# The third channel group of a depthwise convolution moved from TensorE to GpSimd

## The reference

```
val, gate = split(conv_in)                    # 512 channels each
c = val * sigmoid(gate)                       # the gated product
c = depthwise_conv(c, dw_w, width 31, causal) + dw_b
c = silu(layernorm(c, ln_g, ln_b))
yb = c @ w_conv_out
merged = sigmoid(gate_a) * ya + sigmoid(gate_b) * yb      # ya: state-space branch
h = h + merged @ w_out
```

## Time and profile before

| | |
|---|---|
| median of 3 runs | 1172.03 us (1171.83 to 1173.54) |
| profiled execution, its own time | 1168.89 us |
| its span, first to last instruction | 1167.1 us |
| TensorE busy | 990.0 us, 85% |
| VectorE busy | 320.3 us, 27% |
| ScalarE busy | 131.2 us, 11% |
| GpSimd busy | 14.9 us, 1%, 26 instructions |
| memory traffic | 434.87 MB, mean 373 GB/s |
| mean granted TensorE clock | 0.932 |

### The profile page before, as it was taken

How to read it: one execution, slowest core, us unless ns; L and a number is a source line. 1 busy time by engine, 2 the same in 40 slices (tenths; PEclk the granted TensorE clock), 3 DMA queues, 4 the chain that set the end, 5 groups by cost and what they waited for, 6 DMA issues and landing times.

```text
span 1167.1 us, 23860 instructions
## 1 busy us (share of the span) xinstructions
PE 990.0 (85%) x10044; PEld 462.9 (40%) x10045; DVE 320.3 (27%) x949; ACT 131.2 (11%) x292; POOL 14.9 (1%) x26
## 2 busy tenths in 40 slices
PE   8999999999966667689999997699776997977695
PEld 6887886433422222224444332243222342422242
DVE  5999943421211111112212211122111211111112
ACT  2211230500000000000000000000000000000002
POOL 1111000000000000000000000000000000000000
PEclk9999999999998887879999998799878999997898
DMA  9763687695999999997999999999999999999994
GB/s 260 233 169 110 224 331 287 251 424 233 427 427 424 429 424 427 426 427 301 422 411 399 426 426 427 426 425 427 426 425 426 426 426 426 426 426 428 425 426 195
DMA packets 69355, 434.87 MB, mean 373 GB/s; under 512 B 15232, under 2 KB 31552, under 8 KB 36560
## 3 DMA queue, kind: packets, MB, share of 16 engines
q1 hardware_dynamic: 69184, 434.41, 90.9%
q10 hardware_dynamic: 144, 0.09, 0.1%
HBM read 431.69 MB, written 1.05 MB: 371 GB/s over the span
## 4 chain that ended last, share of the span: by engine, by line
PE 45%; DMA 41%; DVE 9%; SPq 3%; issue 2%; ACT 0%; ACTq 0%; DVEq 0%
DMA ring<-in_w_gate_up 24%; PE ps L1478 17%; DMA ring<-in_w_down 13%; PE ps L1491 8%; DMA early<-in_w_gate_up 3%; PE ps L1444 3%; PE ps L1362 2%; PE ps L1413 2%; PE ps L1224 2%; PE ps L1435 2%; PE ps L1467 2%; SPq L369 2%; SPq L366 1%; PE ps L1460 1%; PE ps L1378 1%
## 5 line engine op out<-in xcount | busy, mean ns | idle before, releaser
L1478 PE MATMUL ps<-ring,base 128*32 128x512 f32 x2208 | 294.3, 674 | 115.8 <-DMA ring<-in_w_gate_up 99.4
L1478 PEld LDWEIGHTS ps<-ring,base 128*32 128x32 f32 x2208 | 74.1, 117 | 307.2 <-issue 156.3
L1491 PE MATMUL ps<-ring,base 128*32 128x256 f32 x2944 | 177.5, 381 | 11.5 <-DMA ring<-in_w_down 11.1
L1491 PEld LDWEIGHTS ps<-ring,base 128*32 128x32 f32 x2944 | 89.7, 110 | 101.6 <-issue 33.4
L1131 DVE TENSOR_SCALAR base<-ps 128x256 f32<-128x256 f32 x46 | 19.5, 425 | 379.6 <-PE ps L1478 379.6
L1224 PE MATMUL ps<-ring 128*128 128x256 f32 (+1 forms) x448 | 103.4, 390 | 0.0
L1224 PEld LDWEIGHTS ps<-ring 128*128 128x128 f32 x448 | 84.9, 192 | 15.8 <-issue 1.4
L697 ACT ACTIVATE base<-base 128x256 f32<-128x256 f32 x46 | 19.1, 416 | 628.5 <-DVE base L1131 628.5
L1087 DVE TENSOR_TENSOR base<-ps,base 128x256 f32<-128x256 f32 x47 | 20.0, 425 | 203.3 <-PE ps L1453 203.3
L1478 PE MATMUL ps<-early,base 128*32 128x512 f32 x368 | 52.4, 694 | 16.3 <-DMA early<-in_w_gate_up 16.3
L1478 PE MATMUL ps<-late,base 128*32 128x512 f32 x368 | 50.1, 666 | 13.6 <-DMA late<-in_w_gate_up 13.6
(11 more groups left out here) (323 smaller groups left out, 687.4 us busy)
## 6 DMA issues: line engine op xcount, KB each, us to landing
ring<-in_w_gate_up SPq DMA_DIRECT2D x96, 2048.0 KB, 38.8
ring<-in_w_down SPq DMA_DIRECT2D x63, 2048.0 KB, 40.6
late<-in_w_gate_up SPq DMA_DIRECT2D x16, 2048.0 KB, 40.5
early<-in_w_gate_up SPq DMA_DIRECT2D x16, 2048.0 KB, 39.8
ring<-in_w_in SPq DMA_DIRECT2D x14, 1024.0 KB, 7.8
ring<-in_w_out SPq DMA_DIRECT2D x4, 1024.0 KB, 13.0
ring<-in_w_s_lin SPq DMA_DIRECT2D x2, 1024.0 KB, 6.1
ring<-in_w_s_gate SPq DMA_DIRECT2D x2, 1024.0 KB, 5.4
```

What stands on the lines that cost most here:

```text
L1478: ins = nc.tensor.matmul(ps[BS * q:BS * q + BS, 0, :].rearrange("p (a c) -> p a c", a=2), xT[:, k % 2, k // 2, :], row[:, :, QW * q:QW * q ...
L1491: ins = nc.tensor.matmul(ps[BS * q:BS * q + BS, 1, 0:QW], actT[:, n % 2, n // 2, :], row[:, out_cols(q)], start=(n == 0), stop=(n == KT - ...
```

## The change

`PM` goes from 3 to 2, so groups 0 and 1 stay on TensorE, and `conv(2)` and `tap_matrices(2)` are gone. Group 3 stays on VectorE. Group 2 is computed by GpSimd right behind the gated product: one `tensor_scalar` for tap 0 with the bias, and for each of the other 30 taps a `tensor_scalar` into one of two scratch tiles and a `tensor_tensor` that adds it to the sum, each waiting for the one before. `tap_matrices(1)` comes after all of it in GpSimd's list. The table of taps now has two groups in a buffer of its own, and its two transfers are issued before SyncE waits for `glu`, ahead of the 16 copies. `mean()` also waits for the new semaphore `conv_pool`.

```diff
-PM = MT - 1
+PM = MT - 2
...
+        taps_sb = sb("taps_sb", [P, 2 * TAPS + 2 * S])
...
-        taps = view(rX2, 128, TAPS)
+        taps = view(taps_sb, 0, 2, TAPS)
+        tapped = [view(taps_sb, 2 * TAPS + S * n, S) for n in range(2)]
...
-                   20: [("conv", 1)], 21: [("out", 1), ("in", 3), ("conv", 2)], 23: [("out", 2)],
+                   20: [("conv", 1)], 21: [("out", 1), ("in", 3)], 23: [("out", 2)],
...
+            for n in range(2):
+                sp.dma_start(taps[:, n, :], T["conv_dw_w"][0].rearrange("j o c -> (j o) c")[
+                    :, (PM + n) * P:(PM + n + 1) * P].rearrange("j p -> p j"), allow_slow_non_contiguous=True
+                             ).then_inc(taps_in, 16)
             sp.wait_ge(glu, 1)
...
             load(N_IN - 1)
-            sp.dma_start(taps, T["conv_dw_w"][0].rearrange("j o c -> (j o) c")[:, PM * P:].rearrange("j p -> p j"),
-                         allow_slow_non_contiguous=True).then_inc(taps_in, 16)
...
             nc.gpsimd.tensor_tensor(cin[:, :, HALO:HALO + L], cin[:, :, HALO:HALO + L], cgate, ALU.mult
                                     ).then_inc(glu, 1)
+            pool.wait_ge(taps_in, 32)
+            pool.wait_ge(glu, 1)
+            acc = cacc[:, PM, :]
+            link(nc.gpsimd.tensor_scalar(acc, cin[:, PM, 0:S], taps[:, 0, 0:1], colp[:, 12 + PM:13 + PM], ALU.mult, ALU.add))
+            for j in range(1, TAPS):
+                link(nc.gpsimd.tensor_scalar(tapped[j % 2], cin[:, PM, j:j + S], taps[:, 0, j:j + 1], None, ALU.mult))
+                nc.gpsimd.tensor_tensor(acc, acc, tapped[j % 2], ALU.add).then_inc(conv_pool, 1)
+                pool.wait_ge(conv_pool, j)
             for m in range(1, PM):
                 pool.wait_ge(conv_mm, m)
                 tap_matrices(m)
...
-            dve.wait_ge(taps_in, 16)
+            dve.wait_ge(taps_in, 32)
...
             def mean():
                 pe.wait_ge(conv_sb, PM)
                 pe.wait_ge(conv_dve, 1)
+                pe.wait_ge(conv_pool, TAPS - 1)
```

More of the change, by code:

```diff
@@ L275, in build @@
                                                                   sem("tap_in"), sem("shifts"), sem("cw_ready"))
-        taps_in, conv_dve = sem("taps_in"), sem("conv_dve")
+        taps_in, conv_dve, conv_pool = sem("taps_in"), sem("conv_dve"), sem("conv_pool")
         scales, dn_tail = sem("scales"), sem("dn_tail")
@@ L962, in _ @@
             recurrence(3)
-            dve.wait_ge(taps_in, 16)
+            dve.wait_ge(taps_in, 32)
             dve.wait_ge(glu, 1)
-            last = cacc[:, PM, :]
-            link(nc.vector.tensor_scalar(last, cin[:, PM, 0:S], taps[:, 0:1], colp[:, 12 + PM:13 + PM], ALU.mult, ALU.add))
+            last = cacc[:, MT - 1, :]
+            link(nc.vector.tensor_scalar(last, cin[:, MT - 1, 0:S], taps[:, 1, 0:1], colp[:, 11 + MT:12 + MT], ALU.mult,
+                                         ALU.add))
             for j in range(1, TAPS):
-                ins = nc.vector.scalar_tensor_tensor(last, cin[:, PM, j:j + S], taps[:, j:j + 1], last, ALU.mult, ALU.add)
+                ins = nc.vector.scalar_tensor_tensor(last, cin[:, MT - 1, j:j + S], taps[:, 1, j:j + 1], last, ALU.mult,
+                                                     ALU.add)
                 if j < TAPS - 1:
```

## The result

The change makes the kernel slower: 1215.49 us in the median of 4 runs (1213.87 to 1219.73) against 1172.2 (now four runs too), a ratio of 1.0374 with a 95% interval of 1.0348 to 1.0399. That is 43.3 us more; 40 were forecast, and the time lies inside the range.

A forecast was written before the change was run, and what follows sets the result against it. Two nearly equal chains, on VectorE and TensorE, were taken to bound the mixer. A delay of 38.7 us through `conv(1)` plus 1.6 for the clock restart made 40.3 on 1172.0: 1212 us, range 1196 to 1232.

The forecast's parts named there:

- The step that decides: On TensorE, `conv(1)` waits for `tap_matrices(1)` behind GpSimd's taps: start at 142.7 instead of 100.26, everything later 38.7 us late.
- What the change removes: `conv(2)` leaves TensorE, 3.6 us worth nothing by itself; `tap_matrices(2)` goes, with one hold of 1.70 us on VectorE.
- The start of the taps: GpSimd's taps need both tables of taps, forecast to be there at 73.5 us, bounds 66 and 76.
- The price of a GpSimd `tensor_scalar`: Each 128x256 tap instruction of this form: 0.40 us, bounds 0.21 and 0.63, from a select at 8 and 128 elements.
- What VectorE loses: GpSimd and VectorE exclude each other in turns, 61 against 61: VectorE loses 25.5 us, bounds 14.6 and 38.
- The sum of the two: Taps on GpSimd end after VectorE's own 41.8 us plus 25.5 us of holds from 73.5, at 140.8 us.
- The second rival, dear GpSimd instructions: GpSimd's form with a factor per partition costs 1.0 us more in each of 31: 1243 us; chance 0.12.
- The restart: TensorE, idle for over 30 us before `conv(1)`, resumes at a slower clock: 1.6 us added, bounds 0 and 3.2.
- 1 to 1 to the end: The experts on TensorE follow without slack, nothing can be fetched ahead, so all of the delay reaches the end.
- The literal lock: Shared ports held for whole GpSimd instructions: VectorE would lose full durations, 29.2 us, and the end would be 1216, not 1212.

The follow-up runs named there:

- the run with tap 0 alone: The changed kernel with taps 1 to 30 of the GpSimd group left out, so part of the computation is missing; 1170.38 us, with 3 blocks of experts more.
- the run with `tensor_tensor`: The changed kernel with each tap's product as a tensor_tensor with the tap broadcast along the row, in place of tensor_scalar; 1209.55 us, ratio 1.0324.
- the matrices first: The changed kernel with a matrix buffer per TensorE group and group 1's tap matrices written ahead of GpSimd's 61 tap instructions; 1182.09 us, ratio 1.0098.
- the convolution last: The changed kernel with the second convolution before the last projection tile in TensorE's and ScalarE's order, not before the ninth from the end; 1187.05 us, ratio 1.0133.
- both edits: The changed kernel with group 1's tap matrices ahead of the taps and the product of each tap as a tensor_tensor; 1188.96 us, ratio 1.0148.
- 98 products: The changed kernel with 98 matrix products, result overwritten, run on TensorE while it waits for the second convolution's matrices; 1214.23 us, ratio 1.0358.
- 104: The changed kernel with 104 overwritten matrix products on TensorE during its wait for the second convolution's matrices; 1214.03 us, ratio 1.0364.

## Why the prediction was right, point by point

- **The step that decides** held: the second convolution behind GpSimd's taps, TensorE idle for 44.93 us, everything behind it later. It started at 145.87 us, forecast 142.7. Two edits that take only the queue away (1182.09 and 1187.05) remove 33 and 28 of the 43 us. `out(0)`, forecast some 6 us late, waited 0.70.
- **What the change removes** held. 3.6 us less on TensorE are worth almost nothing; in the run with tap 0 alone 2.19 of them are waited away at `out(3)`.
- **The start of the taps** held: 72.0, forecast 73.5. Unforeseen was that SyncE needed 5.95 us to issue the two tables, not 1.4, so the copies for `shifted` began at 65.77 instead of 63.18. Their cover hid it: `conv(0)` started at 92.49 without a wait for them.
- **The price of a GpSimd `tensor_scalar`** failed: 0.93 us against 0.40 and an upper bound of 0.63. A select at 8 and 128 elements was no guide to it. The `tensor_tensor` was 0.64, at the upper bound. Alone the 61 instructions take 53.3 us (0.83 + 30 x 1.57 + 60 x 0.09), not 35.3.
- **What VectorE loses** failed too, the other way: 8.9 us against 25.5 and a lower bound of 14.6. (Its third recurrence ends at 124.0; in the run with tap 0 alone at 116.7, with a hold of 1.6 in it.) Nineteen pairs began in that time, not 30, and each took 0.47 us, forecast 0.84, lower bound 0.48. So the price of a pair lay at the lower bound, and the number of pairs beside VectorE was too high. Turns are what the run with `tensor_tensor` shows, where both engines end together (135.7 and 136.2). With a `tensor_scalar` in the pair GpSimd does most of the waiting: 71.8 us from first to last less 53.3 alone is 18.5 us, against the 8.9 of VectorE.
- **The sum of the two** came out near by chance: 41.8 + 25.5 = 67.3 us of forecast chain against 71.8. The forecast had GpSimd as the quick partner of a slowed VectorE; it was a slow one beside a VectorE little disturbed. The second rival, dear GpSimd instructions, was half true: the form was 0.53 us dearer than priced, but its surplus was not added on top of 25.5 us of holds, as I had it.
- **The restart** held in kind: 2.57 us on the convolution (6.23 - 3.66), 1.6 forecast, bounds 0 and 3.2. That a second piece of slow clock could follow at the step to the experts, 3.7 us in the profiled execution, was not foreseen.
- **1 to 1 to the end** held. Within one execution the second block of experts is 47.9 us late and the end 48.1. The mark is 44.2 us late and the median 43.3; they come from different executions. In the other runs that keep the computation whole and wait ahead of the mark, the two agree within 3 us: 12.1 and 10.7 with the matrices first, 16.8 and 15.6 with the convolution last, 35.3 and 38.1 with `tensor_tensor`, 18.7 and 16.3 with both edits, 42.9 and 41.6 with 98 products, 41.6 and 42.1 with 104.
- **The literal lock** of the Trainium skill ("SBUF — State Buffer", Who interferes with whom), a hold for the whole instruction, is not what these instructions show: VectorE lost 0.35 us to a `tensor_tensor` of about 0.62, and the pair with a `tensor_scalar`, 1.57 us long, took 0.47 from it. The share lost is not fixed either: it was 1.70 of 1.94 us for the one pair that the prediction took its ratio of 0.88 from.

## What to carry to other kernels

Before work is given to an idle engine, look at what stands behind it in that engine's list and who waits for it: here one instruction of 1.93 us, queued behind 61 others, cost 33 of 43 us. Ask next whether the engine that is relieved sets the end at that place; here it would have waited for another anyway. And a right total can hide two wrong prices, so the steps are to be checked one by one; when a run changes the data, check first that it still does the same amount of work.

## What the runs showed of the hardware that was not expected

- A GpSimd `tensor_scalar` of 128x256 float32 takes 0.93 us, 0.85 with a constant factor; a `tensor_tensor` of the same size takes 0.64, and at its shortest 0.61 as the product with a broadcast factor.
- Beside a busy VectorE the `tensor_scalar` takes up to 2.96 us. The one from 101.84 to 104.80 let the rest of one VectorE instruction and the whole of the next through, which ran its usual 1.28 us. What it waits for is open.
- Behind 42.5 us of unbroken matrix products and an idle spell of 2.66 us the convolution took 5.35 us at a granted clock of 0.68; without the spell it took 3.66 at 1.00. A longer spell did not always cost more: 6.58 us behind 16.67, 5.21 behind 32.61 (the product as a `tensor_tensor`), 6.23 behind 44.93.
- Two element-wise transposed loads of 15.5 KB held SyncE's queue for 5.95 us when they were issued right behind a 1 MB load; one of them, issued later in the kernel before, held it for 0.70.
